# Mixer stage of a two-block network on one Trainium2 core: the attention products, the triangular solve and its inverse are queued nine or eleven product steps later, and the recurrence loads its activation table once

## The chip, the cores and the metric

One core of a Trainium2 chip runs the whole network. Its engines are named as the profile names them: PE (TensorE) with its weight loads PEld, DVE (VectorE), ACT (ScalarE), POOL (GpSimd) and SP (SyncE, which here only issues weight transfers). Each engine works through its own queue of instructions in order and waits on semaphores. The metric is the device time of one execution in microseconds, the median of several; less is better.

## The reference

The input is 512 tokens of 1024 channels. It goes through a differential-attention layer and then through a second block: a gated MLP, a token mixer, another gated MLP and a last normalisation. The change touches the token mixer only. Cut to what matters, with 8 heads of 128 channels, 512 tokens and chunks of 64 in the reference (the kernel uses chunks of 128, which gives the same recurrence):

```python
proj = h @ mix_w_in                      # xp, q, k, v, z, b, a, gates
qkv = silu(causal_depthwise_conv([q, k, v], conv_w))        # 4 taps
qh, kh = l2_normalize(q) * 128**-0.5, l2_normalize(k)
beta, g = sigmoid(b), -exp(a_log) * softplus(a + dt_bias)
a_mat = strict_lower(beta * (kc @ kc.T) * decay)            # per chunk
u, w = solve(I + a_mat, [beta * vc, beta * exp(gc) * kc])
qk = lower(qc @ kc.T * decay)
for each chunk:                                             # S: 128x128 per head
    v_new = u - w @ S
    o = (q * exp(gc)) @ S + qk @ v_new
    S = S * exp(g_last) + k_dec.T @ v_new
yb = (rms_norm(o) * dn_norm_g * silu(z)) @ dn_proj
out = (sigmoid(g_pool) * ya + sigmoid(g_dn) * yb) @ mix_w_out
```

Everything is float32.

## The kernel before, in words

**Products.** A matrix product is cut into tiles of 128 output channels by 512 tokens, and a tile into steps of 128 input channels. The weights of a tile (128x1024, "a slot") are brought in by SP, split by ACT into a high part `wH` (L1632) and by DVE into the rest `wL` (L1275), and a step is three matmuls: high by high, high by low, low by high (L993, L994, L996). There are three split slots, so the split that ACT and DVE make after tile n ends belongs to tile n+3, and PE can be up to two tiles ahead of them.

**One list of steps, five queues.** `Plan` writes one list of operations by hand, and each engine goes through that list and takes its own part of each operation, in the same order. Where an operation stands in the list therefore decides what is queued in front of it on every engine. In the mixer the order is set by a counter, `clock[0]`, which goes up by one after each product step; this text calls its value the step number. `at(n, f)` puts operation `f` into the list once the counter has reached n. Where no product step follows, the counter runs on by itself.

**The stage with the convolutions.** Its 288 steps are, in order: four tiles of k (steps 1 to 32), a gate tile and four steps of `pool_out` (33 to 44); the same with k heads 4 to 7 (45 to 88), q 0 to 3 (89 to 132) and q 4 to 7 (133 to 176); then the eight v tiles with a gate tile and a `pool_out` after each second of them. For each tile of q, k or v:

- at the tile's end ACT copies the bank out (L1799) and splits the next slot (L1632), DVE splits too (L1275);
- one step later DVE does the four taps (`conv_taps`, L1508 to L1513);
- six steps later ACT does SiLU and, for q and k, the square (L1804, L1811).

Each group of four heads has a "session" that begins `end` steps in (32, 76, 120, 164; the first two for k, the others for q):

- `end`+10 to +13: `l2_sum`, PE's sum over channels of the squares (L1123), which waits for ACT's square;
- +15: `l2`, ACT's Ln and Exp of the four (L1817, L1821), with a table load;
- +16 to +22, k only: `prep_x`, the decays (PE L1137, DVE L1527, ACT L1828 and L1829);
- +23: `l2_end`, DVE's scaling of the four heads (L1519);
- +25 to +31: `prep_k` (PE L1144, products of k with k) or `prep_q` (PE L1151, k with q), one head every two steps. They wait for `l2_end`. Two steps behind each, DVE takes the result: `prep_k_end` (L1534, then POOL multiplies by beta, L1955) or `prep_q_end` (L1539, L1541).

At step 112 POOL sends the eight heads' matrices through DRAM into another layout (`sol_send`, L1960 and L1962; it first waits for all eight POOL products). Thirty `solve` operations (DVE, L1550 and L1553, two instructions each), one every two and a half steps, begin at step 126 and end at step 199. At step 200 POOL sends the result back (`sol_back`, L1965 and L1968; it waits for the last `solve`). From step 224 five `inverse` operations per half (PE L1159 to L1204, with copies on ACT and DVE), three steps apart, complete the inverse; the first waits for `sol_back`. PSUM banks 3 to 7 are handed out in turn, in the order in which operations come into the list. `v_turn` (L1129), 12 steps behind the end of each v tile, is PE's transposition of v.

**The recurrence** follows, four rounds (`t`) over two groups of four heads (`g`) with no product steps in between, then `zd` tiles. A round is, in list order: `rec_r` (not in round 0), `rec_v`, the head sums of the round before, `rec_s` (not in the last), the head ends of the round before, `rec_k` of the next round, `rec_o`. `head_sum` is a sum on PE (L1260) and then on ACT a table load (L1862), Ln (L1864) and Exp (L1866); `head_end` is one DVE instruction (L1607). `rec_o` on PE (L1252, L1254) needs the bank that `head_end` of the same group frees.

Of the kernel before, what the change touches and what calls it, by code (L numbers as in the profile page):

```python
# [109 lines left out]
def src(name, col, nk=8, row=0, cols=128):  # L110
    return (name, row, nk, col, cols)
# [19 lines left out]
class Plan:  # L131
# [13 lines left out]
    def sig(self, name):  # L145
        self.count[name] = self.count.get(name, 0) + 1
        return self.count[name]
# [4 lines left out]
    def add(self, what, **d):  # L152
        self.steps.append((what, d))
        return d
# [282 lines left out]
    def mixer(self):  # L437
        sig, add = self.sig, self.add
# [18 lines left out]
        t = Tile("ba", src("mix_w_in_2", 4608, cols=16), wk.take()[1], "h", ("bd", 1), n=n)  # L457
# [10 lines left out]
        def at(tick, fn, *a):  # L468

            n_ev[0] += 1  # L470
            events.append((tick, n_ev[0], fn, a))
# [114 lines left out]
        def session(end, which, hs):  # L586

            l2s = []
            for j, h in enumerate(hs):
                at(end + 10 + j, l2_sum, h, l2s)  # L590
                if which == "k":
                    at(end + 16 + 2 * j, prep_x, h)
                    at(end + 25 + 2 * j, prep_k, h)
                else:
                    at(end + 25 + 2 * j, prep_q, h)
            at(end + 15, l2, which, l2s)
            at(end + 23, l2_end, which, l2s)

        session(32, "k", range(4))
        session(76, "k", range(4, 8))  # L600
        session(120, "q", range(4))
        session(164, "q", range(4, 8))
        at(7, pool_mid, 2)
        at(11, lambda: add("decays", bank=wk.take()[1]))
        at(15, pool_mid, 3)
        at(112, lambda: add("sol_send", pa2=8))
        for k in range(1, 31):
            at(124 + (5 * k) // 2, lambda k=k: add("solve", k=k))
        at(200, lambda: add("sol_back"))
        for g in range(2):  # L610
            for j, step in enumerate(("t", "p5", "y5", "p6", "y6")):
                at(224 + 16 * g + 3 * j, inverse, g, step)
        po = iter(range(8))
        for which in "kq":
            for g in range(2):
# [30 lines left out]
        for t in range(4):  # L646
            if t > 0:
                for g in range(2):
                    d = dict(g=g, t=t, ks=sig("ks"), rr=[sig("rr") for _ in range(4)], ur=ur[g], st=st[g])
# [14 lines left out]
            for g in range(2):  # L664
                om[g] = sig("om")
                d = dict(g=g, t=t, at=ro.take()[1], om=om[g], vv=vv[g], hq=sig("hq"), hn=sig("hn"), i=(2 * t + g) % 4)
# [44 lines left out]
def model_kernel(nc: bass.Bass, wst, wfd, small_d, const_d, x_d, xd, modd, out_d):  # L711
# [3 lines left out]
    with ExitStack() as ctx:  # L715
# [27 lines left out]
        def C(name, a=0, b=None):  # L743
            at, n = CONST[name]
            return cst[:, at + a:at + (n if b is None else b)]
# [8 lines left out]
        def b4(x, t):  # L754
            return x[:, 128 * t:128 * t + 128]
# [128 lines left out]
        def blocks(x, p, n, c, m):  # L884

            return x[p:p + n, :].rearrange("p (x c) -> p x c", c=128)[:, :, c:c + m]
# [9 lines left out]
        def half8(g):  # L896
            return AT8[:, 2048 * g:2048 * g + 2048]
# [730 lines left out]
        def _(e):  # L1628
            w = Waits(e)

            def hi_of(dst, x, name):
                e.activation(dst, x, ACT.Copy).then_inc(s[name], 1)  # L1632

            for what, d in steps:
                if what == "split":
                    if d["j"] < len(slots):
                        j = d["j"]
# [48 lines left out]
                elif what == "out_qk":  # L1686
                    t, d = d["t"], d["d"]
# [23 lines left out]
                elif what == "turnw":  # L1711
                    h, kb = d["h"], d["kb"]
                    if kb < 3:
                        at, n = sum(128 * (4 - j) for j in range(kb)), 128 * (4 - kb)
# [15 lines left out]
                elif what == "out_ze":  # L1730
                    t, d = d["t"], d["d"]
# [8 lines left out]
                elif what == "out_z":  # L1740
                    t, d = d["t"], d["d"]
# [10 lines left out]
                elif what == "out_gate":  # L1752
                    t, f, j = d["t"], ff[d["f"]], d["j"]
# [4 lines left out]
                elif what == "out_up":  # L1758
                    f, j = ff[d["f"]], d["j"]
                    w.wait_ge(s["fu"], d["fu"])  # L1760
                    hi_of(f["aH"][j], f["ac"][j % 2], "ah")
                elif what == "out_pool":
                    t, g = d["t"], d["g"]
# [4 lines left out]
                elif what == "pool_mid":  # L1768
                    g = d["g"]
# [17 lines left out]
                elif what == "out_gp":  # L1787
                    t = d["t"]
# [5 lines left out]
                elif what == "out_conv":  # L1794
                    t, d = d["t"], d["d"]
# [4 lines left out]
                elif what == "conv_act":  # L1800
                    h = d["h"]
# [3 lines left out]
                elif what == "conv_sq":  # L1805
                    h = d["h"]
# [15 lines left out]
                elif what == "v_turn":  # L1822
                    w.wait_ge(s["dvt"], d["dvt"])
                    e.activation(VnD[d["h"]], ps[d["bank"]][:], ACT.Copy).then_inc(s["dvn"], 1)
                elif what == "prep_x":
                    h = d["h"]
                    w.wait_ge(s["px2"], d["px2"])
                    e.activation(QK[h], QK[h], ACT.Exp).then_inc(s["pxs"], 1)  # L1828
                    e.activation(VnD[h], ps[d["bank"]][:], ACT.Exp).then_inc(s["px1"], 1)  # L1829
                elif what == "inv_t":  # L1830
                    w.wait_ge(s["l2n"], 16)
                    for hh in range(4):
                        w.wait_ge(s["it"], d["it"][hh])
                        e.activation(Xb[hh], ps[d["banks"][hh]][:], ACT.Copy).then_inc(s["ix"], 1)
                elif what == "inv_y5":
                    w.wait_ge(s["i6"], d["i6"])
                    e.activation(blocks(X4, 32, 32, 0, 32), ps[d["banks"][1]][32:64, :].rearrange("p (x c) -> p x c", c=32),
                                 ACT.Copy).then_inc(s["ixx"], 1)
                elif what == "inv_p6":
                    w.wait_ge(s["i7"], d["i7"][0])  # L1840
                    e.activation(P6[64:128, 0:512], ps[d["banks"][0]][64:128, :], ACT.Copy).then_inc(s["i7a"], 1)
                elif what == "inv_y6":
                    w.wait_ge(s["i8"], d["i8"][0])
                    e.activation(blocks(half8(d["g"]), 0, 64, 64, 64)[:, 0:8, :],
                                 ps[d["banks"][0]][0:64, :].rearrange("p (x c) -> p x c", c=64), ACT.Copy).then_inc(s["yua"], 1)
                elif what == "rec_k":
                    g, t = d["g"], d["t"]
                    w.wait_ge(s["kdt"], d["kdt"])
                    w.wait_ge(s["ba"], 7)
                    w.wait_ge(s["i8"], 4)  # L1850
                    if d["sn"]:
                        w.wait_ge(s["sn"], d["sn"])
                    for hh in range(4):
                        col = 8 * t + 4 * g + hh
                        e.activation(b4(Kdr[g], hh), b4(ps[d["bank"]], hh), ACT.Copy, scale=ekd[:, col:col + 1]).then_inc(s["kd"], 1)
                elif what == "rec_o":
                    if d["hn"] > 4:
                        w.wait_ge(s["hn"], d["hn"] - 4)
                    w.wait_ge(s["om"], d["om"])
                    e.activation(Xb[d["i"]], ps[d["at"]][:], ACT.Square).then_inc(s["hq"], 1)  # L1860
                elif what == "head_sum":
                    e.preload_act_table_set("natural_log_exp_and_others")  # L1862
                    w.wait_ge(s["hm"], d["hm"])
                    e.activation(Xb[d["i"]], ps[d["bank"]][:], ACT.Ln, bias=C("eps")).then_inc(s["hl"], 1)  # L1864
                    w.wait_ge(s["hl"], d["hl"])
                    e.activation(Xb[d["i"]], Xb[d["i"]], ACT.Exp, scale=-0.5).then_inc(s["hx"], 1)  # L1866
                elif what == "mix_out":
                    w.wait_ge(s["om"], d["om"])
                    w.wait_ge(s["m1"], 8)
                elif what == "out_zd":  # L1870
                    t, h = d["t"], d["h"]
                    w.wait_ge(s["slot"], t.done)
                    w.wait_ge(s["om"], 8)
                    e.activation(zs[h], ps[t.bank][:], ACT.Silu).then_inc(s["zds"], 1)
                elif what == "zd_out":
                    w.wait_ge(s["zdm"], d["zdm"])
                    hi_of(oH[d["h"]], zs[d["h"]], "oh")
                elif what == "out_gd":
                    t, d = d["t"], d["d"]
                    w.wait_ge(s["slot"], t.done)  # L1880
                    w.wait_ge(s[d["free"][0]], d["free"][1])
                    e.activation(zb3[d["i"]], ps[t.bank][:], ACT.Tanh, scale=0.5).then_inc(s["gds"], 1)
                elif what == "out_dn":
                    d = d["d"]
                    w.wait_ge(s["dn2"], d["dn1"])
                    hi_of(mH[d["c"]], zb3[d["i"]], "mh")
# [149 lines left out]
```

## Time and profile before

| what | value |
|---|---|
| median of 3 runs | 1967.96 us (1966.72 to 1968.32) |
| the profiled execution's own time | 1967.84 us |
| its span in the trace | 1966.0 us |
| PE, DVE, ACT, POOL busy | 97%, 46%, 40%, 6% |
| chain that ended last, by engine | PE 88%, DVE 6%, ACT 4%, DMA 1% |
| stage with the convolutions / recurrence in the trace | about 1056 to 1363.7 us / 1363.7 to 1410.5 us |

Times in the rows are counted from the span's start. A row of the timeline gives start, duration, engine, line, operation, tiles written and read, and in brackets how long the engine had been idle and what released it; rows of the same line that follow each other are merged (x2). The granted clock (PEclk) is TensorE's, as a share of full speed.

Mean durations in this stage, from the groups by line and the timeline:

| instruction | ns |
|---|---|
| DVE: wL split L1275; taps of one tile L1508, L1511 x2, L1513 together | 1223; 2760 |
| DVE: L1519, L1534, L1539, L1541 each | 683 |
| DVE: L1550 and L1553, mean of 30 | 327 and 332 |
| ACT: wH split L1632; SiLU L1804 and square L1811 each | 1049; 631 |
| ACT: table load; four Ln L1817; four Exp L1821; L1828 with L1829 | 1283; 2290; 2090; 1000 |
| POOL: product with beta L1955 | 1092 |
| start to start on PE: pool_out step or l2_sum; two product steps with one head's prep_x or prep_k | 860; 2280 |

### The profile page before, as it was taken

What the parts mean: (1) busy time and instruction counts of PE and PEld (TensorE: products, weight loads), DVE (VectorE), ACT (ScalarE), POOL (GpSimd) and SP (SyncE); (2) the same over time, 40 slices, a digit from 0 to 9 for tenths busy, and PEclk for the clock granted to TensorE, in tenths of its full rate; (3) what the DMA queues carried; (4) which work ended last, traced back from release to release, by engine and by line L of the source; (5) the groups of instructions that cost most, each with busy time, mean ns of one, the idle gap of its engine ahead of it and who ended that gap; (6) DMA issues with size and microseconds to landing.
All of it is one profiled execution on the core that took longest, in us unless ns stands there. A gap on an engine that the chain in (4) does not pass through costs nothing.

```text
span 1966.0 us, 22086 instructions
## 1 busy us (share of the span) xinstructions
PE 1903.2 (97%) x8907; PEld 1465.0 (75%) x8907; DVE 904.8 (46%) x1615; ACT 787.8 (40%) x1262; POOL 125.6 (6%) x148
## 2 busy tenths in 40 slices
PE   7999999999999899999998899899999999999997
PEld 4666666666788788888876677677788878888886
DVE  4656555665542433333226555845433453333322
ACT  5555555555642323222224544334632332222221
POOL 0111111110001000000000011000000100000000
PEclk9999999999999999999998999999999999999999
DMA  5334333332243132222313212221022323232321
GB/s 210 144 138 148 140 140 140 144 144 88 76 141 106 65 107 97 97 97 89 100 61 139 86 59 81 70 87 55 12 97 97 141 76 104 92 103 94 91 98 62
DMA packets 56524, 201.94 MB, mean 103 GB/s; under 512 B 6478, under 2 KB 6934, under 8 KB 55784
## 3 DMA queue, kind: packets, MB, share of 16 engines
q1 hardware_dynamic: 44616, 158.32, 23.9%
q0 software_dynamic: 11808, 42.21, 5.9%
q8 instruction: 71, 1.16, 0.2%
q14 instruction: 29, 0.24, 0.0%
HBM read 195.23 MB, written 5.28 MB: 102 GB/s over the span
## 4 chain that ended last, share of the span: by engine, by line
PE 88%; DVE 6%; ACT 4%; issue 1%; DMA 1%; DVEq 0%; SPq 0%; ACTq 0%
PE ps L993 25%; PE ps L996 24%; PE ps L994 24%; PE ps L1044 2%; PE ps L1034 2%; PE ps L1080 2%; PE ps L1068 2%; PE ps L1116 1%; DVE wL L1275 1%; ACT wH L1632 1%; PE ps L1056 1%; PE ps L1017 1%; PE ps L1144 1%; DMA wr<-wst 1%; DVE a L1511 0%
## 5 line engine op out<-in xcount | busy, mean ns | idle before, releaser
L993 PE MATMUL ps<-hH,wH 128*128 128x512 f32 (+1 forms) x1640 | 681.1, 415 | 19.9 <-DVE hL L1315 12.3
L996 PE MATMUL ps<-hH,wL 128*128 128x512 f32 (+1 forms) x1640 | 646.7, 394 | 0.7 <-DVE wL L1275 0.7
L994 PE MATMUL ps<-hL,wH 128*128 128x512 f32 (+1 forms) x1640 | 645.7, 394 | 0.0
L1275 DVE TENSOR_TENSOR wL<-wr,wH 128x1024 fp32r<-128x1024 f32 (+2 forms) x285 | 344.1, 1208 | 580.8 <-ACT wH L1632 580.7
L993 PEld LDWEIGHTS ps<-hH,wH 128*128 128x128 f32 (+1 forms) x1640 | 311.6, 190 | 124.7 <-issue 55.2
L1632 ACT ACTIVATE wH<-wr 128x1024 fp32r<-128x1024 f32 (+2 forms) x285 | 295.2, 1037 | 272.2 <-PE ps L996 252.0
L994 PEld LDWEIGHTS ps<-hL,wH 128*128 128x128 f32 (+1 forms) x1640 | 312.0, 190 | 69.7 <-issue 10.8
L996 PEld LDWEIGHTS ps<-hH,wL 128*128 128x128 f32 (+1 forms) x1640 | 311.0, 190 | 69.8 <-DVE wL L1275 2.1
L993 PE MATMUL ps<-gffn,wH 128*128 128x512 f32 x352 | 136.9, 389 | 0.0
L994 PE MATMUL ps<-gffn,wH 128*128 128x512 f32 x352 | 136.9, 389 | 0.0
L996 PE MATMUL ps<-gffn,wL 128*128 128x512 f32 x352 | 136.9, 389 | 0.0
L1710 ACT ACTIVATE a<-a,tiny 128x128 f32<-128x128 f32 (+3 forms) x128 | 71.0, 555 | 141.9 <-DVE tiny L1359 141.9
L1632 ACT ACTIVATE gffn<-affn 128x512 fp32r<-128x512 f32 x44 | 27.8, 632 | 197.8 <-DVE affn L1426 197.8
L1426 DVE TENSOR_TENSOR affn<-ps,affn 128x512 f32<-128x512 f32 x44 | 30.4, 691 | 110.7 <-PE ps L996 110.7
L1757 ACT ACTIVATE affn<-ps 128x512 f32<-128x512 f32 x44 | 26.3, 598 | 133.6 <-PE ps L996 133.6
L996 PEld LDWEIGHTS ps<-gffn,wL 128*128 128x128 f32 x352 | 66.1, 188 | 13.8
L993 PEld LDWEIGHTS ps<-gffn,wH 128*128 128x128 f32 x352 | 66.1, 188 | 13.8
L994 PEld LDWEIGHTS ps<-gffn,wH 128*128 128x128 f32 x352 | 66.1, 188 | 13.5
L993 PE MATMUL ps<-g,wH 128*128 128x512 f32 x192 | 74.8, 389 | 0.0
L996 PE MATMUL ps<-g,wL 128*128 128x512 f32 x192 | 74.7, 389 | 0.0
L994 PE MATMUL ps<-g,wH 128*128 128x512 f32 x192 | 74.7, 389 | 0.0
L1921 POOL TENSOR_TENSOR affn<-affn 128x512 f32<-128x512 f32 x12 | 18.5, 1542 | 704.8 <-ACT affn L1659 704.8
(279 smaller groups left out, 1937.1 us busy)
## 6 DMA issues: line engine op xcount, KB each, us to landing
wr<-wst SPq DMA_DIRECT2D x268, 512.0 KB, 3.4
a<-wfd POOLq DMA_DIRECT2D x54, 512.0 KB, 4.6
xT<-wfd POOLq DMA_DIRECT2D x18, 512.0 KB, 6.8
wr<-wst SPq DMA_DIRECT2D x16, 384.0 KB, 3.0
xT<-xin SPq DMA_DIRECT2D x8, 256.0 KB, 4.8
xT<-xin SPq DMA_DIRECT2D x2, 1024.0 KB, 6.4
xsave<-xT SPq DMA_DIRECT2D x1, 2048.0 KB, 9.1
c<-wfd POOLq DMA_DIRECT2D x8, 256.0 KB, 2.9
```

The lines of the kernel that those rows point to most:

```text
L993: e.matmul(o, hi, xh[k], start=k == 0, stop=False)
L994: e.matmul(o, hi, xl[k], start=False, stop=False)
L996: i = e.matmul(o, lo, xh[k], start=False, stop=k == t.nk - 1)
L1034: e.matmul(b[:], m, v, start=True, stop=True).then_inc(s["sum"], 1)
L1044: i = e.matmul(ps[d["banks"][m]][:, a["at"]:a["at"] + n], qn[h % 2][64 * m:64 * m + 64, 128 * qb:128 * qb + 128], kn[h % 2][64 * m:64 * m ...
L1068: i = e.matmul(b[:, 512 - n:512], b4(Vn[h % 3], kb), WT[:, at:at + n], start=kb == 0, stop=kb == 3)
L1080: i = e.matmul(ps[7][32 * j:32 * j + 1, :], csil[:, k:k + 1], ada_buf[a % ADA_BUFS][:, 512 * (j % 2):512 * (j % 2) + 512], start=k == 0, s ...
L1275: e.tensor_tensor(dst, x, hi.bitcast(F32), ALU.subtract).then_inc(s[name], 1)
L1426: e.tensor_tensor(v, ps[t.bank][:], f["sg"][j % 2], ALU.mult).then_inc(s["fu"], 1)
L1632: e.activation(dst, x, ACT.Copy).then_inc(s[name], 1)
L1710: e.activation(v, v, ACT.Exp, bias=mx[:, m:m + 1], accum_out=rsum[:, m:m + 1]).then_inc(s["ex"], 1)
L1757: e.activation(f["sg"][j % 2], ps[t.bank][:], ACT.Silu).then_inc(s["fg"], 1)
```

## The change

The products of `prep_k` stand nine steps later (+34 instead of +25) and those of `prep_q` eleven (+36); the DVE and POOL parts behind them move along. `sol_send`, the thirty `solve`, `sol_back` and the ten `inverse` operations stand nine steps later. Nothing else in the list moves: `l2_sum`, `l2`, `prep_x`, `l2_end`, the convolutions and `v_turn` stay at their steps. In the recurrence ACT's table load before the head sums is issued only for round 0, group 0, so once instead of eight times. No operation on data is added or taken away.

```diff
                 if which == "k":
                     at(end + 16 + 2 * j, prep_x, h)
-                    at(end + 25 + 2 * j, prep_k, h)
+                    at(end + 34 + 2 * j, prep_k, h)
                 else:
-                    at(end + 25 + 2 * j, prep_q, h)
+                    at(end + 36 + 2 * j, prep_q, h)
...
-        at(112, lambda: add("sol_send", pa2=8))
+        at(121, lambda: add("sol_send", pa2=8))
         for k in range(1, 31):
-            at(124 + (5 * k) // 2, lambda k=k: add("solve", k=k))
-        at(200, lambda: add("sol_back"))
+            at(133 + (5 * k) // 2, lambda k=k: add("solve", k=k))
+        at(209, lambda: add("sol_back"))
         for g in range(2):
             for j, step in enumerate(("t", "p5", "y5", "p6", "y6")):
-                at(224 + 16 * g + 3 * j, inverse, g, step)
+                at(233 + 16 * g + 3 * j, inverse, g, step)
...
                 elif what == "head_sum":
-                    e.preload_act_table_set("natural_log_exp_and_others")
+                    if d["t"] == 0 and d["g"] == 0:
+                        e.preload_act_table_set("natural_log_exp_and_others")
```

## Rows read from the trace of the kernel before

**Rows 1.** Waits of PE, 1050 to 1365 us: total, times, longest

```profile
PE ps L1151 <- DVE a L1519: 8.7, 2, 5.2
PE ps L1144 <- DVE o L1519: 4.4, 1, 4.4
PE ps L1144 <- DVE a L1519: 3.9, 1, 3.9
PE ps L1123 <- ACT a L1811: 1.0, 1, 1.0
```

**Rows 2.** Stretches of PE: length, busy (instructions), granted clock, DMA share, GB/s

```profile
1123.05:1127.45 4.40, 0.03 (x1) 0.93 0.29 111
1127.45:1133.70 6.25, 6.25 (x23) 0.51 0.00 0
1172.10:1176.04 3.94, 0.01 (x1) 0.82 0.28 110
1176.04:1181.40 5.36, 5.36 (x19) 0.50 0.01 3
1216.61:1220.17 3.56, 0.00 (x1) 0.83 0.44 147
1220.17:1225.80 5.63, 5.63 (x20) 0.50 0.00 0
1261.23:1266.40 5.17, 0.00 (x0) 0.70 0.31 101
1266.40:1270.10 3.70, 3.70 (x13) 0.50 0.00 0
```

**Rows 3.** Timeline: two product steps, and the end of the first wait

```profile
1087.93 0.39 PE L993 MATMUL ps<-hH,wH 128*128 128x512 f32 x1
1088.61 0.39 PE L993 MATMUL ps<-hH,wH 128*128 128x512 f32 x1
...
1126.62 2.48 DVE L1519 SCALAR_TENSOR_TENSOR o<-o,a 128x512 f32<-128x512 f32 x4
```

**Rows 4.** Timeline: from one split on DVE to the next, and a sum of squares

```profile
1097.86 1.22 DVE L1275 TENSOR_TENSOR wL<-wr,wH 128x1024 fp32r<-128x1024 f32 x1 [2.80 <-ACT wH L1632]
...
1099.51 1.54 DVE L1511 SCALAR_TENSOR_TENSOR o<-c,sml,o 128x512 f32<-128x512 f32 x2
...
1104.63 1.22 DVE L1275 TENSOR_TENSOR wL<-wr,wH 128x1024 fp32r<-128x1024 f32 x1 [2.79 <-ACT wH L1632]
...
1110.08 1.10 PE L1123 MATMUL ps<-a,cst 128*128 128x512 f32 x2 [0.99 <-ACT a L1811]
```

**Rows 5.** The solve: last POOL products, its start, DVE's stretch, PE at step 173

```profile
1190.20 2.06 POOL L1955 TENSOR_TENSOR a<-a,tiny 128x512 f32<-128x512 f32 x2 [2.80 <-DVE a L1534]
...
1205.78 0.09 DVE L1548 MEMSET a<- 128x32 f32 x1 [2.70 <-DMA a<-dsol]
...
1205.78:1282.60 76.82, 59.40 (x120) 0.91 0.19 62
...
1244.94 1.88 PE L1116 MATMUL ps<-o,c 128*128 128x512 f32 x4
```

**Rows 6.** Timeline: the way back from DRAM and the first transposes

```profile
1288.04 3.15 POOL L1968 DMA_DIRECT2D a<-dsol  x4 [4.56 <-issue]
...
1297.40 1.03 PE L1159 MATMUL ps<-cst,a 128*128 128x128 f32 x8
```

**Rows 7.** Timeline: a pair of taps beside a POOL product

```profile
1137.97 1.22 POOL L1955 TENSOR_TENSOR a<-a,tiny 128x512 f32<-128x512 f32 x1 [6.62 <-DVE a L1534]
1138.33 2.21 DVE L1511 SCALAR_TENSOR_TENSOR a<-c,sml,a 128x512 f32<-128x512 f32 x2
```

**Rows 8.** Timeline of the recurrence: round 2 and the last round

```profile
1393.04 1.40 DVE L1607 SCALAR_TENSOR_TENSOR o<-ps,sml,a 128x512 f32<-128x512 f32 x2
...
1403.58 1.28 ACT L1862 ACT_TABLE_LOAD   x1
...
1407.06 0.49 PE L1252 MATMUL ps<-a,o 128*128 128x128 f32 x2 [0.61 <-DVE o L1607]
```

## The prediction, written before the changed kernel was run

> **What bounds the kernel now.** I read the page's chain first: PE holds 88% of it, so only what makes PE wait or run slowly counts. Then the waits of PE in the stage that the change touches [rows 1]: besides one sum of squares (1.0 us) they are four waits for DVE's `l2_end`: 4.4, 3.9, 3.6 and 5.2 us, 17.0 together (the two on L1151 make 8.7). Each stands before a session's first `prep_k` or `prep_q`. Then the granted clock stretch by stretch [rows 2]: it falls to 0.5 (1.2 of 2.4 GHz) after each wait and stays there for 6.25, 5.36, 5.63 and 3.70 us of work. Half of each is loss: 3.1 + 2.7 + 2.8 + 1.9 = 10.4 us. The four late `l2_end` cost 27.4 us.
>
> Why late: with taps in play, split, taps, SiLU, square, copy and split of the next slot form a ring through DVE and ACT. It takes 6.78 us per tile (1097.86 to 1104.63), 2.8 of them DVE's wait for ACT [rows 4], while PE's eight steps take 8 x 0.68 = 5.4 us [rows 3]. PE is carried by its two tiles of lead until the table load, Ln, Exp and decays come on top.
>
> **Products nine or eleven steps later.** At step 57 PE stands at 1123.05. Nine steps at 0.68 bring it to 1129.2, and `l2_end` lets it go at 1127.45 [rows 2]: margin 1.7 us, wait gone. What is late next, followed through (durations of the table):
>
> - *Session 2.* The ring's split after step 60 is at 1132.0 (table load, SiLU, square, copy and split behind the decays end at 1127.9). Three ring turns, plus 0.6 for the `prep_k_end` that now stands ahead of a tile's taps, plus 0.7 for POOL beside it (below): 1153.7 at step 84. Then ACT's 1.05 + 1.28 + 2.29 + 2.09 + 2.0 + 0.5: split after step 96 at 1163.0; `l2_end` comes 6.0 behind and frees PE 0.8 later, at 1169.8. PE, free of the first 7.5 us of loss, needs it at 1170.7. Margin 0.9: gone too. The other three `prep_k_end` of a session fall into DVE's 2.8 us wait for ACT and cost nothing.
> - *Session 3.* The ring gives splits at 1174.4, 1181.1, 1189.2 (with 1.3 for `prep_k_end` and POOL) and 1196.0. The taps of the last q tile end at 1193.1, and the sum of squares can start 1.5 us after them (1.48 in the trace), at 1194.5. PE wants it at 1193.3 (step 133): **a new wait of 1.2 us**. `prep_q` at step 156 is then at 1211; `l2_end` frees it at 1209.7: gone, margin 1.4.
> - *The solve.* The last POOL product ends near 1190.1 instead of 1192.3; from there to the first solve the trace has 13.5 us [rows 5], so it starts at 1203.6 instead of 1205.8. DVE reaches it at about 1197.6 and stands 6 us (2.7 now). From there DVE has no slack: before, it was busy for 59.4 of 76.8 us up to the last solve [rows 5], and PE's two waits that go took 13 of the rest. Up to the taps of the last q tile (step 165) DVE has 4 splits (4.6 us back to back), 4 taps (11.0), `l2_end` (2.4), 4 `prep_q_end` (4.8), 13 solves (8.2) and 0.7 of waiting: 1203.6 + 31.7 = 1235.3, sum of squares possible at 1236.8.
> - *Session 4.* PE ends step 172 at 1244.94 [rows 5] less 20.5 (three waits with their clock) plus 1.2 = 1225.7; four `pool_out`, three sums and a product later, at 1232.4, it needs that sum. **New wait of 4.4 us**, in place of 1.0. The clock fell after all four waits of 3.6 to 5.2 us and not after 1.0 us [rows 1, 2], so I add 2.6 us, the mean of the four. `l2_end` is then ready at 1251 to 1252; PE reaches step 200 at 1254 to 1256: the fourth wait is gone.
>
> The groups: 27.4 - 1.2 - (4.4 - 1.0) - 2.6 = **20.2 us gained**. Without a new wait it would be 27.4 + 1.0 = 28.4, the lower end in time. The upper: if each session pays again what one does now at its sums, nothing is gained.
>
> **Solve and inverse nine steps later.** By the same count the last solve ends at 1268 to 1269 instead of 1282.6. In the trace the last of `sol_back` is issued at 1291.2 [rows 6] and the issues of this kind land 3.0 us later, 11.6 after the solve's end; PE transposes at 1297.4 without a wait, 3.2 of slack. After: back at 1280 to 1281, PE at step 233 at 1283 to 1286. Hidden, with 2 to 5 us left; if the solve ended 5 us later, it would be paid one for one. POOL's feed of the gate weights now stands ahead of `sol_back` instead of behind it and has its own two buffers: nothing. SP's queue is not touched. The second half's inverse now runs beside a gate tile, the first half's beside taps as the second's did, without a wait in the trace [rows 1]: 0, at most 1 us either way. `v_turn` of v0 and v1 now comes into the list among the `prep_q`, so banks change hands otherwise; five banks turn and each was free two steps behind its use: 0.
>
> **One table load.** Seven loads of 1.28 us go, 9.0 us of ACT. In rounds 1 and 2 they do not reach PE: both `head_end` start only when DVE is through with the states, back to back at 1393.04 [rows 8]. In the last round DVE has no states, and the load between the groups delays group 1: Exp, `head_end`, then PE's `rec_o`, which stood 0.61 us [rows 8]. PE's group 0 ends then anyway, so of 1.28 only **0.6 us** comes through. The loads of the last two sums lie beside `zd` products: nothing. Ends: 0 and 1.3.
>
> **A rule against it.** A pair of taps takes 2.21 us beside a POOL product [rows 7], 1.54 without [rows 4]. I took this 0.67 once per k session (1.3 in all, contained above), for only the first `prep_k_end` has taps behind it. The GPSIMD Engine Reference of the Trainium skill, section 1, lists POOL's memory interfaces as shared with VectorE, with contention for DVE instructions with two SBUF inputs; by it every product that meets taps or a split pays. If all eight did, DVE would be 6 x 0.67 = 4.0 us later.
>
> **The sum.** 20.2 + 0.6 = 20.8. The profiled execution took 1967.84 us, its span 1966.0 and 1.84 around it; that is 0.12 below the median of 1967.96, so they may be taken as one. 1967.84 - 20.8 = **1947.0 us**.
>
> **Rivals.**
>
> *A: the whole gain.* DVE keeps up, the sums of squares wait no longer than now. For it: it needs only 4.4 us less work on DVE before step 165, and DVE was idle 17 of 77 us. Against: that idle time was PE's waits. 1967.84 - 28.4 - 0.6 = 1938.8.
>
> *B: the waits come back elsewhere.* All eight POOL products meet DVE, the ring is 4.0 us later; sessions 2 and 3 lose their margins of 0.9 and 1.4, with a half clock each: 4.0 + 2 x 2.6 on top = 1956.2; with one of them 1951 to 1953. For it: the margins are thin. Against: three of four products fall into DVE's 2.8 us wait.
>
> *C: slower, by the way through DRAM.* The solve starts nine steps later (6.1 us) and DVE's pace stays today's: with 3.3 us more standing before it and 4.0 for POOL its end is 1282.6 + 6.1 + 3.3 + 4.0 = 1296.0, back at 1307.6. Step 233 of the old trace is at 1297.4 + 5 x 0.68 + 3.4 + 0.5 = 1304.7. So PE, having gained nothing, would wait 2.9 us with 2.6 of half clock: 1967.84 + 5.5 - 0.6 = 1972.7. It decides once the solve ends after 1293. Against: DVE was idle only because PE was.
>
> *D: the loads are put back* because another function's table is set in between: 1947.6. Against: all eight groups between Exp and the next Ln hold only copies and squares, with no load of their own.
>
> **Chances.** The forecast's own mechanism (one or two new waits at the sums, 1943 to 1950) 0.50 (D, 0.03, lies in it), A with its surroundings (below 1943) 0.22, B (1950 to 1962) 0.23, gain lost down to no change 0.02, C 0.03. Range 1938 to 1955: it takes in A to its end and most of B, and leaves out some 0.15. Faster by over 0.2% (3.9 us, about what a measurement tells from no change) 0.95, within 0.2% 0.02, slower 0.03.
>
> **What would show it.** PE's waits for L1519 gone at L1144 and L1151; granted clock 1.0 around steps 57, 101, 145, 189; in their place waits of L1123 for ACT L1811, about 1.2 us at step 133 and 4.4 at step 177 with the clock at 0.5 behind it; DVE over 90% busy between first and last solve, DVE's wait at L1548 near 6 us; no wait at L1159; one load at L1862 and PE's 0.61 before the last group gone, other rounds the same length to 0.1 us. Wrong would be: waits for L1519 that stay (then the ring itself is slower), a wait at L1159 (the solve's end, not PE, leads), or a recurrence shorter by more than 1.3 us.

## The result, and the profile after

| kernel | us, median of 4 (lowest to highest) | profiled run, span | granted clock |
|---|---|---|---|
| before, on the same chip | 1967.34 (1963.18 to 1968.32) | 1967.84, 1966.0 | 0.984 |
| changed | 1945.40 (1943.36 to 1946.77) | 1946.77, 1944.9 | 0.989 |

The ratio is 0.9897 (95% interval 0.9885 to 0.9909): faster by 1.0%, where 1947.0 us was forecast. Between the two profiled runs (the forecast's sum starts from the one of before) it is 21.07 us against 20.8.

Below, "stage" is the time from the start of step 41 (PE's first L1116 there) to the first matmul of the recurrence (PE L1212), the stretch in which all moved steps lie. It shrinks from 261.52 to 241.91 us. The recurrence, from there to the next product step, shrinks from 46.74 to 45.88 us. The last 0.6 us lie ahead of step 41, where nothing was changed and where the runs differ by more than that (step 41 begins between 1100.8 and 1103.4 us). In kernel.py of after, lines behind 1862 are one higher. Times in two traces can be compared only by their distance to step 41, which after starts 0.63 us earlier (1101.59 against 1102.22).

First the waits of PE in the kernel after, 1050 to 1345 us (waited for: total, times, longest), which answer to [rows 1]:

```profile
PE ps L1123 <- ACT a L1811: 6.3, 4, 2.9
PE ps L993 <- ACT wH L1632: 1.6, 1, 1.6
PE ps L996 <- DVE wL L1275: 0.5, 1, 0.5
PE ps L1212 <- ACT o L1824: 0.2, 1, 0.2
```

No wait for `l2_end` (L1519) and none at the inverse (L1159) is left. The L993 and L996 waits stood before too. Instead the sums of squares wait four times. Here they are in after's timeline, at steps 45, 89, 133 and 177 (in square brackets the wait and its releaser); the first was there before [rows 4], the other three are new:

```profile
1109.41 1.10 PE L1123 MATMUL ps<-a,cst 128*128 128x512 f32 x2 [0.95 <-ACT a L1811]
...
1152.35 1.10 PE L1123 MATMUL ps<-a,cst 128*128 128x512 f32 x2 [1.25 <-ACT a L1811]
...
1195.28 1.10 PE L1123 MATMUL ps<-a,cst 128*128 128x512 f32 x2 [1.24 <-ACT a L1811]
...
1236.14 2.05 PE L1123 MATMUL ps<-a,cst 128*128 128x512 f32 x2 [2.87 <-ACT a L1811]
```

After's stretches of PE (length, busy, granted clock, DMA share, GB/s) answer to [rows 2]. In before the clock was at 0.5 behind each of the four waits. Here it is 1.00 at the places of the first three (and of the fourth); it is 0.50 once, behind the last new wait:

```profile
1126.00:1130.00 4.00, 4.00 (x24) 1.00 0.00 0
1169.00:1173.00 4.00, 4.00 (x23) 1.00 0.00 0
1209.00:1213.00 4.00, 4.00 (x23) 1.00 0.00 0
1233.23:1236.14 2.91, 0.04 (x1) 0.87 0.27 90
1236.14:1242.00 5.86, 5.86 (x12) 0.50 0.27 89
```

After's timeline of the solve answers to [rows 5, 6]: the last POOL products, DVE's start and its wait for DRAM, the end of the last q taps, the last solve, the way back on POOL's queue, the first transposes without a wait:

```profile
1186.92 3.06 POOL L1956 TENSOR_TENSOR a<-a,tiny 128x512 f32<-128x512 f32 x3 [2.80 <-DVE a L1534]
...
1201.55 0.09 DVE L1548 MEMSET a<- 128x32 f32 x1 [3.12 <-DMA a<-dsol]
...
1233.92 0.75 DVE L1513 SCALAR_TENSOR_TENSOR a<-c,sml,a 128x512 f32<-128x512 f32 x1
...
1268.58 0.21 DVE L1553 TENSOR_TENSOR a<-a 128x30 f32<-128x30 f32 x1
...
1270.81 0.57 POOL L1966 DMA_DIRECT2D dsol<-a  x1 [8.47 <-issue]
...
1274.24 2.37 POOL L1969 DMA_DIRECT2D a<-dsol  x3 [2.87 <-DMA dsol<-a]
...
1285.02 1.91 PE L1159 MATMUL ps<-cst,a 128*128 128x128 f32 x16
```

and DVE in the stretch from the first solve on (length, busy, instructions):

```profile
1201.55:1270.80 69.25, 59.34 (x119) 0.95 0.23 72
```

In the recurrence's last round (after's timeline of ACT) the second Ln stands directly behind the first group; before, a load lay there [rows 8]:

```profile
1381.98 0.69 ACT L1865 ACTIVATE a<-ps,cst 128x512 f32<-128x512 f32 x1 [3.84 <-PE ps L1260]
1382.70 0.63 ACT L1867 ACTIVATE a<-a 128x512 f32<-128x512 f32 x1
1383.24 0.67 ACT L1865 ACTIVATE a<-ps,cst 128x512 f32<-128x512 f32 x1
```

### The profile page after: what moved, and what is told of

The parts are those of the page before. It is cut to its first block, busy times and chain, and to the rows that moved or that the text cites. A ratio compares the mean times of both kernels' runs of the same rounds, so it can differ in the third digit from the quotient of the medians.

```text
span 1944.9 us, 22080 instructions
## 1 busy us (share of the span) xinstructions
PE 1894.6 (97%) x8907; PEld 1457.9 (75%) x8907; DVE 906.1 (47%) x1615; ACT 778.2 (40%) x1255; POOL 125.3 (6%) x148
## 4 chain that ended last, share of the span: by engine, by line
PE 86%; DVE 7%; ACT 6%; issue 1%; DMA 1%; DVEq 0%; SPq 0%; ACTq 0%
PE ps L993 24%; PE ps L996 24%; PE ps L994 24%; PE ps L1044 2%; PE ps L1034 2%; PE ps L1080 2%; PE ps L1068 2%; DVE wL L1275 1%; ACT wH L1632 1%; DVE a L1511 1%; PE ps L1056 1%; PE ps L1116 1%; PE ps L1017 1%; DMA wr<-wst 1%; DVE a L1513 0%
## 5 line engine op out<-in xcount | busy, mean ns | idle before, releaser
L993 PE MATMUL ps<-hH,wH 128*128 128x512 f32 (+1 forms) x1640 | 679.6, 414 | 19.8 <-DVE hL L1315 12.3
L996 PE MATMUL ps<-hH,wL 128*128 128x512 f32 (+1 forms) x1640 | 645.5, 394 | 0.7 <-DVE wL L1275 0.7
L993 PEld LDWEIGHTS ps<-hH,wH 128*128 128x128 f32 (+1 forms) x1640 | 310.9, 190 | 124.4 <-issue 55.5
L996 PEld LDWEIGHTS ps<-hH,wL 128*128 128x128 f32 (+1 forms) x1640 | 310.3, 189 | 69.6 <-DVE wL L1275 2.1
L993 PE MATMUL ps<-gffn,wH 128*128 128x512 f32 x352 | 136.9, 389 | 0.0
L996 PE MATMUL ps<-gffn,wL 128*128 128x512 f32 x352 | 136.9, 389 | 0.0
L1632 ACT ACTIVATE gffn<-affn 128x512 fp32r<-128x512 f32 x44 | 27.8, 632 | 197.8 <-DVE affn L1426 197.8
L993 PEld LDWEIGHTS ps<-gffn,wH 128*128 128x128 f32 x352 | 66.1, 188 | 13.8
L996 PEld LDWEIGHTS ps<-gffn,wL 128*128 128x128 f32 x352 | 66.1, 188 | 13.6
L993 PE MATMUL ps<-g,wH 128*128 128x512 f32 x192 | 74.8, 389 | 0.0
L996 PE MATMUL ps<-g,wL 128*128 128x512 f32 x192 | 74.7, 389 | 0.0
```

The source lines that it names most:

```text
L993: e.matmul(o, hi, xh[k], start=k == 0, stop=False)
L996: i = e.matmul(o, lo, xh[k], start=False, stop=k == t.nk - 1)
```

## The experiments

Stage, waits, rest and falls are read from one profiled execution of each kernel. The time is that of this execution for before, changed, e1 to e4, e6 and e8, and the median of four for e5, e7, e9, e10 and e11. The before kernel took 1964.53 us (one run) on the chip of the first four, 1964.99 (median of 7) beside e5 to e8 and 1965.90 (median of 7) beside e9 to e11. "Waits" are those of PE at L1123, L1129, L1144, L1151 and L1159 in the stage, "rest" is the stage without them, "falls" how often the clock went to 0.5 in it. All but the falls in us. The chips differ, so the stage tells more than the time.

| kernel | time | stage | waits | rest | falls |
|---|---|---|---|---|---|
| before | 1967.84 | 261.52 | 18.0 | 243.5 | 4 |
| e1 one load | 1963.79 | 260.96 | 18.2 | 242.8 | 4 |
| e2 `prep_q` only | 1954.45 | 249.27 | 11.9 | 237.4 | 3, short ones |
| changed | 1946.77 | 241.91 | 6.3 | 235.6 | 1 |
| e11 changed again | 1946.17 | 241.91 | 6.3 | 235.6 | 1 |
| e3 solve not moved | 1949.16 | 245.33 | 9.7 | 235.6 | 1 |
| e4 solve 18 later | 1945.24 | 238.51 | 5.3 | 233.2 | 0 |
| e5 sums 4 later | 1944.30 | 240.03 | 6.7 | 233.3 | 0 |
| e6 products of POOL small | 1941.92 | 236.33 | 3.8 | 232.5 | 0 |
| e7 products 4 and 9 later | 1944.65 | 241.16 | 7.9 | 233.3 | 0 |
| e8 `prep_q` 10 later | 1944.05 | 240.75 | 7.4 | 233.4 | 0 |
| e9 `prep_k` 4 apart | 1938.49 | 234.68 | 1.7 | 233.0 | 0 |
| e10 and q's sums 2 later | 1937.31 | 233.73 | 1.0 | 232.7 | 0 |

The rest column bears out how the forecast counts: without a fall it is 232.5 to 233.4 us whatever was moved. One fall adds 2.4 against e4, which has the same four waits of PE as the changed kernel (2.2 to 3.1 against all seven kernels without a fall), and the four of before some 10 (10.4 were forecast). So waits and falls make up the stage's difference to within about 1 us.

**e1: the one load alone.** The kernel before with only

```diff
-                    e.preload_act_table_set("natural_log_exp_and_others")
+                    if d["t"] == 0 and d["g"] == 0:
+                        e.preload_act_table_set("natural_log_exp_and_others")
```

> The kernel before with only the table-load edit (one load before the head sums instead of eight). Theory: of seven loads of 1.28 us only the one of the last round reaches PE; the recurrence from PE's first L1212 to the first product step behind it, 46.7 us before, becomes 45.7 to 46.1, all other rounds keep their 13.0 us, PE's 0.61 us wait before group 1's last outputs is gone, the rest of the trace is as before (1967 us). Rival: the loads between Ln groups lie on PE's path in every round, then three rounds shorten by 1.28 each and the stretch falls to about 42.9 us.

The recurrence took 45.88 us, as in the changed kernel; PE's waits in it fell from 4.1 us in four to

```profile
PE ps L1252 <- DVE o L1607: 3.4, 3, 1.4
```

so just the wait of the last round (0.61, [rows 8]) goes. The gain of 0.86 is more than these 0.61: from the last L1254 before the wait to the first behind it, start to start, there are 1.32 us in before (1406.07 to 1407.39) and 0.45 in e1 (1404.08 to 1404.53). A wait costs PE somewhat more than the idle time that its row shows. The middle rounds of the changed kernel stay 12.99 us long (L1220 at 1351.30, 1364.29, 1377.28). So of the 9.0 us of seven loads 0.86 come through, and no more elsewhere: nothing was changed in the stage, and it is within 0.6 us of before's.

**e2: only `prep_q` later.** Before, with

```diff
-                    at(end + 25 + 2 * j, prep_q, h)
+                    at(end + 36 + 2 * j, prep_q, h)
```

> The kernel before with only prep_q moved (end+36). Theory (each wait costs itself plus its half clock): waits 3 and 4 go, 3.6+2.8+5.2+1.9 = 13.5 us; waits 1 and 2 stay (4.4, 3.9 with the clock at 0.5 behind them); DVE, now without PE's pause, is late with the last q taps and PE's wait at step 177 grows from 1.0 to about 2.2 us, with 0 to 3 us of half clock: 1967.8 - 9.3 to 12.3 = 1955.5 to 1958.5. Rival (DVE is the bound of the q sessions once the solve runs, so the wait only moves): wait at step 177 above 6 us, at most 5 us gained, 1963 or more.

The two waits of the k sessions stay (4.4 and 3.9 us), the two of the q sessions are gone, and a wait for the sum of squares stands at step 177, where before had none. The waits of PE in the stage:

```profile
PE ps L1144 <- DVE o L1519: 4.4, 1, 4.4
PE ps L1144 <- DVE a L1519: 3.9, 1, 3.9
PE ps L1123 <- ACT a L1811: 3.6, 2, 2.6
```

and the stretches of PE at step 177 and behind it:

```profile
1242.17:1244.82 2.65, 0.00 (x1) 1.00 0.32 99
1244.82:1246.00 1.18, 1.18 (x3) 0.94 0.00 0
1246.00:1249.00 3.00, 3.00 (x8) 0.50 0.16 60
```

The stage is 12.3 us shorter. Not all of that is the edit: the two k waits, which it does not touch and which are as long as before, had half clock behind them for about 3.0 and 3.4 us instead of 6.25 and 5.36 [rows 2]. From step 129 to the recurrence, where all that the edit moves lies, the kernel is 9.6 us shorter (163.0 before, 153.4 here), within the 9.3 to 12.3 expected; the time is 1 us below the 1955.5 to 1958.5 expected, as the two k waits cost less. Moving a product group saves its wait and its half clock, and what was hidden by it comes out later.

**e3: the solve and the inverse at their old distance to the steps (nine earlier than in the changed kernel).**

```diff
-            at(133 + (5 * k) // 2, lambda k=k: add("solve", k=k))
-        at(209, lambda: add("sol_back"))
+            at(124 + (5 * k) // 2, lambda k=k: add("solve", k=k))
+        at(200, lambda: add("sol_back"))
-                at(233 + 16 * g + 3 * j, inverse, g, step)
+                at(224 + 16 * g + 3 * j, inverse, g, step)
```

> The changed kernel with solve, sol_back and inverse back at their old steps (124+, 200, 224); sol_send must stay at 121. Theory (from the first solve on DVE has no slack, so what stands in its queue before step 165 sets the sum of squares at step 177): DVE reaches the first solve early and waits some 7.5 us instead of 3.1; before the last q tile's taps it then has 3 or 4 more solves, the split of step 128 and one pool_out result behind it, 4.4 us in all, so PE's wait for L1811 at step 177 is about 7.3 us instead of 2.9: time 1950 to 1953, possibly with a wait at the inverse's first transposes. Rival (the ring of split, taps, SiLU, square, copy sets that wait and the solves fit between): wait stays 2.5 to 3.5 us, time within 1 us of the changed kernel (1946).

The timeline of e3 (DVE's first solve, PE's sum at step 177):

```profile
1201.12 0.09 DVE L1548 MEMSET a<- 128x32 f32 x1 [7.98 <-DMA a<-dsol]
...
1239.23 2.04 PE L1123 MATMUL ps<-a,cst 128*128 128x512 f32 x2 [6.28 <-ACT a L1811]
```

and its waits of PE in the stage:

```profile
PE ps L1123 <- ACT a L1811: 9.7, 4, 6.3
```

DVE comes to the solve earlier and stands in front of DRAM for 8.0 us instead of 3.1; what it cannot do meanwhile, the taps of the last q tile, PE pays at step 177: 3.4 us more. The theory wanted 7.3 us of wait and 1950 to 1953 us; the rival that only the ring of split, taps and squares sets step 177, and that the solve does not matter, is false.

**e4: the solve nine steps later still** (`142 + (5 * k) // 2`, `sol_back` 218, inverse from 242).

> The changed kernel with solve, sol_back and inverse another nine steps later (142+, 218, 242). Theory (DVE without slack): 3 or 4 fewer solves (2.7 us) stand before the last q taps, PE's wait at step 177 falls from 2.9 to 0 to 1 us and the clock stays at 1.0 behind it (3.0 us): 1940 to 1943; no wait at the inverse. Rival (the ring sets the wait): it stays above 2 us with the clock at 0.5, time 1945 to 1947.

```profile
1212.07 0.09 DVE L1548 MEMSET a<- 128x32 f32 x1
...
1236.91 1.10 PE L1123 MATMUL ps<-a,cst 128*128 128x512 f32 x2 [1.81 <-ACT a L1811]
```

DVE no longer waits for DRAM, and nine solves stand ahead of the last q taps instead of 13, yet the wait shrinks only from 2.87 to 1.81 us, not to the 0 to 1 expected, and the time is above the 1940 to 1943 expected. So something else is late next; that it is the ring is argued from the list and fits e9, where the wait is 0.73. The stage gains 3.4 us: 1.0 of wait and 2.4 by the clock, which stays at 1.00 behind 1.8 us.

**e5: the sums, the products and the solve later together** (`l2_sum` +14, `prep_x` +20, `l2` +19, `l2_end` +27, `prep_k` +40, `prep_q` +42, `sol_send` 127, solve as in e4).

> The changed kernel with the sums of squares and all that hangs on them four steps later (l2_sum +14, l2 +19, prep_x +20, l2_end +27, prep_k +40, prep_q +42), sol_send at 127, solve at 142+, sol_back 218, inverse 242. Theory: what is left of the loss is PE reaching l2_sum before ACT's square; four steps are 2.7 us, more than the waits of 1.0, 1.3, 1.2 and 1.8 us with the solve 18 steps later. They go, no l2_end wait comes, the clock stays at 1.0. The stage from step 41 to the recurrence (before 261.5, changed 241.9, solve 18 later 238.5 us) takes 233 to 236 us; against the kernel before 26 to 29 us gained, ratio near 0.986. Rival (DVE and ACT together are the bound of the stage by now, the wait moves to l2_end or to a split): stage 238 or more, with waits for L1519 or for wL in place of L1811.

```profile
PE ps L1129 <- ACT o L1804: 3.6, 2, 1.8
PE ps L1159 <- DMA a<-dsol: 1.6, 1, 1.6
PE ps L1123 <- DVE a L1541: 1.5, 2, 1.3
```

The stage was expected at 233 to 236 us and took 240.0. All waits of L1123 for the squares are gone, but three others stand in their place with 6.7 us: `v_turn` for its SiLU, banks that DVE frees late, and the way back from DRAM, which a solve this late no longer fits under the steps. The stage is 1.9 us shorter than the changed kernel's, all of it the fall that is not there. Ratio to before 0.9892 (0.9876 to 0.9908).

**e6: what POOL beside DVE costs.** The changed kernel, in which POOL's product with beta runs over one of 128 columns; most of beta is left out of the matrices.

```diff
-                    e.tensor_tensor(v3(at), v3(at), v3(beta)[:, :, d["h"]:d["h"] + 1].broadcast_to([128, 4, 128]),
+                    e.tensor_tensor(v3(at)[:, :, 0:1], v3(at)[:, :, 0:1], v3(beta)[:, :, d["h"]:d["h"] + 1],
```

> The changed kernel, with POOL's product with beta cut to one column of 512 per chunk and head (the other columns of the matrices stay without beta; the output is not the reference's). Theory (POOL's product slows the DVE instruction beside it): the pair of taps that takes 2.21 us falls to 1.54, the split that takes 2.03 to 1.23, in both k sessions; the ring is 1.5 us shorter in each, PE's waits for L1811 at steps 89 and 133 (1.25 and 1.24) fall to 0 to 0.2; stage 239 to 240 us instead of 241.9. Rival (these two are slow for their own reasons, bank or place): durations and both waits unchanged.

In the groups (busy, mean ns of one | idle before), first the changed kernel from 1100 to 1200 us:

```profile
L1275 DVE TENSOR_TENSOR wL<-wr,wH 128x1024 fp32r<-128x1024 f32 x12 | 16.3, 1359 | 30.5 <-ACT wH L1632 30.5
L1511 DVE SCALAR_TENSOR_TENSOR a<-c,sml,a 128x512 f32<-128x512 f32 x16 | 13.4, 835 | 0.6
```

and e6 in the same stretch:

```profile
L1275 DVE TENSOR_TENSOR wL<-wr,wH 128x1024 fp32r<-128x1024 f32 x12 | 14.7, 1226 | 30.5 <-ACT wH L1632 30.5
L1511 DVE SCALAR_TENSOR_TENSOR a<-c,sml,a 128x512 f32<-128x512 f32 x16 | 12.0, 752 | 0.6
```

Of its waits for the squares two are left, 3.8 us with the 1.0 of step 45. In the timeline the one at step 177, and then a stretch of PE behind it:

```profile
1234.47 1.10 PE L1123 MATMUL ps<-a,cst 128*128 128x512 f32 x2 [2.87 <-ACT a L1811]
```

```profile
1235.00:1236.00 1.00, 1.00 (x5) 1.00 0.00 0
```

The same work on DVE takes 3.0 us less in 100. It is two pairs of taps at 0.67 each and two splits at 0.80 each, and the two waits of 1.25 and 1.24 us at steps 89 and 133 go with it. In the changed kernel's timeline the split that meets POOL in the first k session is this:

```profile
1143.98 3.06 POOL L1956 TENSOR_TENSOR a<-a,tiny 128x512 f32<-128x512 f32 x3 [2.80 <-DVE a L1534]
...
1146.09 2.03 DVE L1275 TENSOR_TENSOR wL<-wr,wH 128x1024 fp32r<-128x1024 f32 x1 [1.00 <-ACT wH L1632]
```

2.03 us instead of the 1.22 of [rows 4]. The wait at step 177 stays at 2.87, but POOL has a part in it all the same. Counted from step 41, PE comes there 2.9 us earlier than in the changed kernel, and the squares come 2.9 us earlier too (134.55 and 131.66 us): the solve, which needs POOL's products, starts 2.6 us earlier. The two shifts hide each other. The stage gains 5.6 us, more than the 2 to 3 expected: 2.5 are waits, and the other 3.1 in the rest column are for the most part the fall, which did not come behind the same 2.87 us.

**e7: the products later by four (k and q alike: `end + 29 + 2 * j`) and no more.**

> The changed kernel with prep_k and prep_q only four steps behind their old place (+29 both), solve and inverse as changed. In the changed trace l2_end was ready 1.6, 1.6, 2.9 and 4.1 us before PE took it; five or seven steps less (3.4, 4.8 us) bring back waits of about 1.8, 1.8, 1.9 and 0.7 us for L1519. Theory (the clock falls only after the longer waits, here after 2.6 us and more, and costs by itself): clock 1.0 behind all four; and as PE comes later by 1.8 us a session, the waits for L1811 at 89, 133 and 177 shrink to 0, 0 and 0 to 1.2 without the fall of the clock (3.0 us). Stage 239 to 243 us, so equal to the changed kernel's 241.9. Rival (each wait of this place brings the half clock, 2.6 us each, or the steps gained and not the waits make the time): stage 248 to 252 us.

```profile
PE ps L1151 <- DVE a L1519: 3.3, 2, 2.0
PE ps L1123 <- ACT a L1811: 1.7, 2, 1.0
PE ps L1144 <- DVE o L1519: 1.7, 1, 1.7
PE ps L1144 <- DVE a L1519: 1.2, 1, 1.2
```

The four waits for `l2_end` are back with 1.2 to 2.0 us instead of 3.6 to 5.2. The clock is 1.00 all along, and step 177 needs only 0.66 us. The time, 1944.65 us (0.9895, 0.9877 to 0.9914), cannot be told from the changed kernel's. So the first four steps bring all of the gain; the last five or seven swap four waits of 6.2 us, and 0.7 at step 177, for three new ones of 5.4 with one fall.

**e8: `prep_q` ten steps later than in the changed kernel** (`end + 46 + 2 * j`).

> The changed kernel with prep_q another ten steps later (+46). Theory (what stands in DVE's queue ahead of the last q taps sets the wait at step 177): four prep_q_end (4.8 us) now stand behind them; PE's wait at 177 falls from 2.9 to 0 to 1 us, where the ring ends it, the clock stays up: stage 236 to 238.5 us instead of 241.9. Rival (only the solves and the late start of the solve matter, or the ring does): wait 2 us or more, stage above 240.

```profile
PE ps L1123 <- ACT a L1811: 3.5, 3, 1.3
PE ps L1123 <- DVE a L1541: 3.2, 2, 2.7
```

At step 177 the wait is for a bank now, which `prep_q_end` (L1541) frees: 2.66 and 0.51 us. With `prep_q_end` out of DVE's way the squares are in time, as the theory said, but PE finds no bank, and the stage is 240.75 us instead of the 236 to 238.5 expected. Moving further gains nothing but a fall that did not come.

**e9: each `prep_k` four steps from the next, the solve later** (`sol_send` 128, solve as in e4).

```diff
-                    at(end + 34 + 2 * j, prep_k, h)
+                    at(end + 36 + 4 * j, prep_k, h)
```

> The changed kernel with prep_k four steps apart instead of two (end+36, +40, +44, +48), sol_send at 128, solve at 142+, sol_back 218, inverse 242. Theory (POOL's product beside a two-input DVE instruction costs DVE 0.7 to 0.8 us each time, and the ring's delay sets the waits at steps 89 and 133): two POOL products at a time fit into DVE's 2.8 us wait for ACT, no split and no pair of taps is slowed, the waits of 1.25 and 1.24 us go as they did without beta; at step 177 some 1.8 us stay as with the solve 18 later, clock 1.0. Stage from step 41 to the recurrence 235.5 to 237.5 us (changed 241.9), about 5 us less than the changed kernel. Rival (spread over more steps they meet other DVE work, or the sums wait for PE's banks): slowed instructions elsewhere, waits at the sums above 1 us each, stage 238.5 or more.

1938.49 us (1937.58 to 1941.02); ratio to before 0.987 (0.9853 to 0.9887). Only two waits are left, the 0.97 of step 45 and 0.73 at step 177 (1.8 were expected), and the stage is 234.7 us, below the 235.5 to 237.5 expected. It is 3.8 us shorter than that of e4, which has the solve at the same steps; so the spacing (with `sol_send` seven steps later) gives this much, and the later solve the other 3.4, mostly by the fall that is not there. Spread out, POOL's products no longer pile up beside the split: between 1100 and 1200 us every split takes 1.22 to 1.23 us and every single L1511 0.75. In e9's timeline the split that was stretched takes

```profile
1144.32 1.22 DVE L1275 TENSOR_TENSOR wL<-wr,wH 128x1024 fp32r<-128x1024 f32 x1 [1.60 <-ACT wH L1632]
...
1145.97 1.54 DVE L1511 SCALAR_TENSOR_TENSOR a<-c,sml,a 128x512 f32<-128x512 f32 x2
```

**e10: e9 with the sums and products of the q sessions two steps later** (`l2_sum` +12, `l2` +17, `l2_end` +25, `prep_q` `end + 38 + 2 * j`).

> As the kernel with products four apart, and in the two q sessions the sums and what hangs on them two steps later (l2_sum +12, l2 +17, l2_end +25, prep_q +38). Theory: PE comes 1.4 us later to the sums of steps 133 and 177, the 1.8 us left there fall to about 0.4 and no new wait comes since prep_q_end still stands before step 174: stage 234.5 to 236.5 us. Rival (DVE is the bound of the q sessions): the wait goes to a bank that prep_q_end frees (L1541) or to v_turn, and the stage stays at that of the products four apart or above it.

```profile
PE ps L993 <- ACT wH L1632: 1.7, 1, 1.7
PE ps L1123 <- ACT a L1811: 1.0, 1, 1.0
PE ps L996 <- DVE wL L1275: 0.5, 1, 0.5
```

1937.31 us (1936.73 to 1938.12), ratio 0.986 (0.9845 to 0.9875). All waits that were not there before are gone: the stage is 27.8 us shorter than before's, close to the 27.4 that the four waits and their clock cost. Its gain of 28.6 us on its chip is about what rival A asked for (29.0), so the whole gain can be had, but not by the change alone.

**e11: the changed kernel again**, unedited, beside e9 and e10.

> The changed kernel again, unedited, on the chip of the two others and timed in five rounds. Expected 0.989 of the kernel before, stage 241 to 242.5 us; the wait at step 177 at 2.9 us again. Whether the clock falls behind it is open: it fell in the first profile after 2.87 us and did not after 2.87 us without beta. If it does not fall, the stage is 239 us.

1946.17 us (1943.47 to 1947.37), ratio 0.9903 (0.9888 to 0.9918). The new waits come back to 0.01 us, with the clock at 0.50 behind the last. On this chip e10 is 8.9 us faster than the change: it beats both kernels.

## Why the prediction was right, and which terms were not

**The four waits go (forecast 27.4 us).** So they did, each with about the margin named or more: at steps 57 and 101 1.6 us (forecast 1.7 and 0.9), at 156 2.9 (1.4), at 200 4.2 (2 to 5). e2 shows that the two of q go without the two of k, and the rest column that the half clock was worth about 10 us.

**The new wait at step 133 (1.2 us)** measured 1.24, and e6 shows that it goes when POOL's product is small. The close number is luck: with the 0.63 us of step 41 added, both PE (1194.67 against 1193.3) and the squares (1195.91 against 1194.5) came 1.4 us later than forecast, for the reason that follows, and the two errors cancel.

**Step 89: the failed step.** "The other three `prep_k_end` of a session fall into DVE's 2.8 us wait for ACT and cost nothing", and POOL's price was taken once per k session. The `prep_k_end` did fall into the wait, but the POOL products that they release did not: they reached the next split and stretched it by 0.80 us (e6). That helped to push session 2 over its edge: a wait of 1.25 us that the forecast did not have. Without the 0.80 there would still be 0.45 of it, as far as sums go: the forecast followed session 2 to its `l2_end` and never asked when PE needs the sum at step 89. e6, which takes both contacts away (1.47 us), has no wait there. It was rival B's mechanism at a small part of its size: two contacts per session instead of one, no fall of the clock. The GPSIMD Engine Reference of the Trainium skill, section 1, says that DVE instructions with two SBUF inputs contend with POOL for shared interfaces. The trace agrees: both forms that slowed, the pair of taps (c and a) and the split (wr and wH), have two such inputs, and L1508, with one, took its usual 0.48 us at 1139.79 beside the same POOL product as the slow pair.

**Step 177, mis-sized: 4.4 us forecast, 2.87 measured.** The chain was as told (e3 with its 8.0 and 6.28 us is the same chain made longer), but two of its terms were off. The way of the matrices through DRAM, from the last POOL product to the first solve, took 11.6 us and not the 13.5 of before (1189.98 to 1201.55), so that DVE stood 3.12 us there instead of 6. And DVE took 33.1 us and not 31.7 from there to the end of the last q taps (1234.67), with 1.9 us of waiting for ACT where 0.7 were booked. With the 0.63 us of step 41 added, PE got the squares at 1236.8, just as forecast. What made the wait smaller is PE: it came at 1233.9 and not at 1232.4, most of it the missed 1.25 us of step 89. e4 adds what the forecast lacked: with nine solves ahead of the taps instead of 13, 1.8 us are still left.

**A slip in the sum.** The forecast booked the wait at 177 "in place of 1.0". The 1.0 of [rows 4] belongs to step 45 and is still there (0.95). The sum should have taken all of the new wait: 19.2 us instead of 20.2, and 1948.0 instead of 1947.0. The 28.4 us of rival A have the same 1.0 too much.

**The fall (2.6 us):** one fall came. By the rest column it cost 2.4.

Put together from the measured terms: 27.4 - 1.25 - 1.24 - 2.87 - 2.4 = 19.6 us; the stage gained 19.6. The missed wait (1.25) and the oversized one (1.5 too much) are nearly one error: as long as DVE sets when the squares of step 177 are ready, what PE loses ahead of it comes off its wait there. That much is the mechanism's doing. The slip of 1.0 has no such excuse: without it the forecast would have been 0.4 us under the stage's gain instead of 0.6 over it, so it cost nothing by luck.

**Solve and inverse.** The last solve ended at 1268.8 (forecast 1268 to 1269), PE came to the transposes at 1285.0 (1283 to 1286) without a wait. From its first solve on DVE was busy for 59.3 of 69.3 us, 86%, not over 90% as named. e5 shows how near the way back is: with the sums later too, PE waited 1.6 us for it. Rival C's mechanism exists; here it had slack.

**The load (0.6 us)** gave 0.86, in the last round alone, as argued; D (the loads put back) is out, as the changed kernel's recurrence has one load. The load took 1.28 us [rows 8], and in the trace of before the next Ln started 1.29 after the load did. ScalarE: Activation LUTs of the Trainium skill, in its section on what a table load costs, adds a drain to each switch to a different set. By the kernel's lines seven of these loads fetch the set already in use; no drain shows behind the one of [rows 8], and no run here tests a switch to another set.

**Left open.** What sets off the fall of the clock (below), and why `sol_back` was issued 2.0 us after the last solve in after and 0.3 in before.

## What to carry to other kernels

Move a consumer that waits only as far as the wait costs more than what the move brings to light: four steps gave as much as nine, because the engine that was late (DVE) had used the waits to catch up. Then look where the moved work lands on the late engine, and on the engine that slows it: spacing the four products of a session (e9, with the solve moved to suit) gave 7.7 us over the change on the same chip, about half of it from the spacing (e9 against e4). To price a schedule, subtract waits from the stage first; a rest that does not come out the same tells of the clock.

## What the runs showed of the hardware

A POOL product with two inputs cost DVE 0.67 us in a pair of taps that takes 1.54 without it and 0.80 us in a split that takes 1.23. In the changed kernel's k session from 1140 us on both losses are a little less than what POOL's product still had to run when the DVE instruction began: 0.88 us (1140.30 to 1141.18) and 0.95 us (1146.09 to 1147.04).

In this stage the clock fell to the lower level in or right behind each wait of 3.5 us or more (four in before, four in e1, two in e2, the 6.28 of e3), and behind none of up to 2.0. In between it went both ways: it fell with 2.65 (e2) and with 2.87 and 2.86 (the changed kernel, twice), not with 2.87 (e6) and 2.66 (e8). Where waits stand close together, shorter ones were enough: ahead of the stage, in before, waits of 1.67 and 0.53 us (PE L993 at 1056.99, L996 at 1058.25) had the clock at 0.5 from 1058.5 to 1062 behind them. And the time at 0.5 differs at the same wait: behind the 4.4 us of step 57 it was 6.25 us in before and about 3.0 in e2, where nothing up to there was changed. So a wait of nearly 3 us can cost 5.3 or 2.9; single runs that differ by 2.4 us in a stage may differ in nothing else.
